# Two transformer blocks, float32, one core: layer 0's scale and shift alone ahead of the context pass, on four 32-column tiles of TensorE; its gate during the context heads

## The reference, cut to what matters

```python
for l in range(DEPTH):                                  # DEPTH = 2
    sh_l, sc_l, g_l = jnp.split(jax.nn.silu(c) @ w_mod[l] + b_mod[l], 3, axis=-1)
    sh_c, sc_c, g_c = jnp.split(jax.nn.silu(c_ctx) @ w_mod[l] + b_mod[l], 3, axis=-1)
    hl = xl * (1.0 + sc_l[:, None, :]) + sh_l[:, None, :]
    hc = xc * (1.0 + sc_c) + sh_c
    parts_c = jnp.split(hc @ w_in[l], SPLIT_POINTS, axis=-1)
    ...                                                 # conv, heads, pooling of ctx and x
    xl_new = _layernorm(DEEPNORM_ALPHA * xl + g_l[:, None, :] * out_l, ln_g[l], ln_b[l])
    xc = _layernorm(DEEPNORM_ALPHA * xc + g_c * out_c, ln_g[l], ln_b[l])
```

## Time and profile before

| what | value |
|---|---|
| time, median of 3 runs | 3728.88 us (3725.71 to 3730.09) |
| span of the profiled execution | 3719.5 us |
| PE busy | 3467.2 us, 93% of the span |
| DVE busy | 2288.1 us, 62% |
| ACT busy | 1303.7 us, 35% |
| DMA moved | 516.21 MB, mean 139 GB/s |

### The profile page before, as it was taken

How to read it: one execution, slowest core, us unless ns; L and a number is a source line. 1 busy time by engine, 2 the same in 40 slices (tenths; PEclk the granted TensorE clock), 3 DMA queues, 4 the chain that set the end, 5 groups by cost and what they waited for, 6 DMA issues and landing times.

```text
span 3719.5 us, 48605 instructions
## 1 busy us (share of the span) xinstructions
PE 3467.2 (93%) x16800; PEld 2732.9 (73%) x16800; DVE 2288.1 (62%) x2909; ACT 1303.7 (35%) x1730; POOL 209.9 (6%) x396
## 2 busy tenths in 40 slices
PE   8699999899999999999799999999997998898996
PEld 2299989678777777878588777767785777687784
DVE  6455565886767764656655566665655888554433
ACT  0145544432334343225522334342326222344323
POOL 1000000000000000110000000000110000000000
PEclk9799999999999999998899999999998999999998
DMA  9844445445223222654554222221652222221231
GB/s 379 267 169 168 166 157 218 143 176 189 105 85 111 99 84 81 234 195 152 187 192 161 105 95 107 104 83 71 217 201 91 80 90 85 80 79 62 103 115 65
DMA packets 95158, 516.21 MB, mean 139 GB/s; under 512 B 11536, under 2 KB 11568, under 8 KB 55760
## 3 DMA queue, kind: packets, MB, share of 16 engines
q1 hardware_dynamic: 51328, 343.95, 25.4%
q0 software_dynamic: 43728, 170.91, 13.3%
HBM read 492.80 MB, written 22.02 MB: 138 GB/s over the span
## 4 chain that ended last, share of the span: by engine, by line
PE 72%; DVE 10%; issue 6%; DVEq 4%; DMA 4%; ACT 3%; ACTq 1%; POOL 0%; SPq 0%; POOLq 0%; PEldq 0%
PE acc L946 20%; PE acc L947 19%; PE acc L948 19%; DVE xy L1739 5%; PE S L1007 3%; PE pv L1041 2%; DVEq L1738 2%; PE S L1136 2%; DVE w_lo L1274 1%; PE misc L1118 1%; PE S L1015 1%; DMA bias_d<-evt 1%; PE S L1009 1%; DMA xy<-in_wm 1%; DVE gates L1321 1%
## 5 line engine op out<-in xcount | busy, mean ns | idle before, releaser
L946 PE MATMUL acc<-h_hi,w_hi 128*128 128x512 f32 (+1 forms) x4736 | 1747.3, 369 | 142.5 <-DVE h_lo L1280 67.6
L947 PE MATMUL acc<-h_lo,w_hi 128*128 128x512 f32 (+1 forms) x4736 | 1713.4, 362 | 0.0
L948 PE MATMUL acc<-h_hi,w_lo 128*128 128x512 f32 (+1 forms) x4736 | 1711.8, 361 | 0.0
L946 PEld LDWEIGHTS acc<-h_hi,w_hi 128*128 128x128 f32 x4736 | 908.5, 192 | 337.4 <-issue 126.2
L948 PEld LDWEIGHTS acc<-h_hi,w_lo 128*128 128x128 f32 x4736 | 909.4, 192 | 135.3
L947 PEld LDWEIGHTS acc<-h_lo,w_hi 128*128 128x128 f32 x4736 | 910.5, 192 | 132.0 <-issue 6.3
L1274 DVE TENSOR_TENSOR w_lo<-raw,w_hi 128x2048 fp32r<-128x2048 f32 x296 | 677.0, 2288 | 270.9 <-ACT w_hi L540 266.0
L540 ACT ACTIVATE w_hi<-raw 128x2048 fp32r<-128x2048 f32 x296 | 564.7, 1908 | 6.9 <-DVEq L1265 6.2
L540 ACT ACTIVATE ev<-acc 128x512 f32<-128x512 f32 (+1 forms) x210 | 110.8, 532 | 1255.9 <-PE acc L948 1222.7
L1321 DVE SCALAR_TENSOR_TENSOR gates<-gates,csil 128x512 f32<-128x512 f32 x568 | 412.2, 750 | 82.8 <-DMA gates<-in_wm 48.1
L1423 DVE TENSOR_REDUCE small<-S 128x2 f32<-128x1536 f32 (+1 forms) x80 | 123.4, 1543 | 309.7 <-PE S L1009 304.4
(11 more groups left out here) (199 smaller groups left out, 2160.2 us busy)
## 6 DMA issues: line engine op xcount, KB each, us to landing
raw<-in_w SPq DMA_DIRECT2D x296, 1024.0 KB, 4.8
gates<-in_wm POOLq DMA_DIRECT2D x216, 512.0 KB, 4.4
xy<-in_wm SPq DMA_DIRECT2D x32, 1024.0 KB, 10.0
x_d<-xy POOLq DMA_DIRECT2D x2, 4096.0 KB, 14.0
vtok<-in_wm POOLq DMA_DIRECT2D x8, 512.0 KB, 7.2
qb<-x_d POOLq DMA_DIRECT2D x16, 256.0 KB, 3.1
kb<-x_d POOLq DMA_DIRECT2D x16, 256.0 KB, 3.8
out_y<-xy POOLq DMA_DIRECT2D x4, 1024.0 KB, 4.1
```

Of the source, the lines that this page charges most:

```text
L946: mm(o, w_hi[:, w], h_hi[:, x], start=n == 0, stop=False)
L947: mm(o, w_hi[:, w], h_lo[:, x], start=False, stop=False)
L948: last = mm(o, w_lo[:, w], h_hi[:, x], start=False, stop=n == len(ks) - 1)
```

## The change

Four things change.

1. **Opening.** The 32 loads of 1 MB now hold scale (16), then shift (16), one block of 128 inputs x 2048 outputs each, from an array of its own, `in_wm0`. For each PE makes four matmuls of 512 columns, one into each quarter of 32 partitions of the same bank (`mod0_step`); the stationary operand is a table `csil0` of 32 columns, of which two hold the vectors and 30 are zero. After 16 steps ACT copies the whole bank out, and four transposes give the columns (`mod0_transposes`). Two weight tiles are loaded ahead of the last eight.
2. **Gate.** Its 16 loads, two per context head, are issued by SP between the loads of weight tiles 0 and 1 of the head, into slots 0 and 1 of `xy`, after a wait that PE has used the slot's last content. PE uses them behind tile 3 of that head; a copy, four transposes and two additions finish it after the last head. PE's loop over the context heads is unrolled. The old path on POOL, DVE and PE is gone.
3. **Bias table.** It is prepared in `kb` and stored from there. POOL issues the store behind the context tokens, as soon as DVE is ready, and DVE waits for it ahead of the context heads; ACT no longer waits.
4. **Rope table.** It is loaded behind the tokens of pass `a`, since its place holds `csil0`.

```diff
+M0_SLOTS = 4
+M0_STEPS = 2 * KT
...
+        csil0 = rope[:, 0:KT * 32]
+        mod0_sums = [S[:, MC * n:MC * (n + 1)] for n in range(2)]
+        mod0_cols = (misc, pv)
+        gate0_row = gates[:, 0:MC]
...
@@ SP
-            def mod0(i):
-                for s in range(4):
-                    sp.wait_ge(m0_used, shown(m0_used, At(s - 3, 4, i)))
-                    sp.dma_start(xy[:, s * D:(s + 1) * D].rearrange("p (t n) -> p t n", t=2),
-                                 A["wm"][bass.ds(i * 8 + 2 * s, 2)].rearrange("t p n -> p t n")).then_inc(m0_landed[s], 16)
-            loop(sp, 0, MOD0_CHUNKS, mod0)
+            for e in range(M0_STEPS):
+                if e == M0_STEPS - 8:
+                    for p in range(2):
+                        load(j_at("cconv", 0, p), w0[p:p + 1])
+                s = e % M0_SLOTS
+                if e >= M0_SLOTS:
+                    sp.wait_ge(m0_used, shown(m0_used, e - M0_SLOTS + 1))
+                sp.dma_start(xy[:, s * D:(s + 1) * D], A["wm0"][e:e + 1]).then_inc(m0_landed[s], 16)
...
+            def chead(i):
+                for p in range(4):
+                    load(j_at("chead", i, p), w0[bass.ds(i * 4 + (16 + p), 1)])
+                    if p == 0:
+                        for s in range(2):
+                            sp.wait_ge(m0_used, shown(m0_used, At(M0_STEPS - 1 + s, 2, i)))
+                            sp.dma_start(xy[:, s * D:(s + 1) * D], A["wm0"][bass.ds(i * 2 + (M0_STEPS + s), 1)])\
+                                .then_inc(m0_landed[s], 16)
+            loop(sp, 0, N_HEADS, chead)
@@ POOL
-                             (evt[0:16, 0:384], A["negmask"])):
+                             (kb[0:16, 0:384], A["negmask"])):
                 pool.dma_start(dst, src).then_inc(consts, 16)
-
-            def gates0(i):
...
-            loop(pool, 0, 4, gates0)
             for dst, src in ((edge[:], A["edge"]),
                              (work[:, 0:KT * CTX].rearrange("p (k t) -> p k t", t=CTX), A["ctxT"])):
                 pool.dma_start(dst, src).then_inc(late_consts, 16)
-            pool.wait_ge(mod_used, shown(mod_used, 4 * MOD_TILES))
-            pool.dma_start(rope, A["rope"]).then_inc(rope_land, 16)
             pool.wait_ge(setup_dve, shown(setup_dve, 3))
             pool.dma_start(bias_d[0:16 * P * 384].rearrange("(h q n) -> h q n", q=P, n=384),
-                           evt[0:16, 0:384].unsqueeze(1).broadcast_to([16, P, 384])).then_inc(bias_st, 16)
+                           kb[0:16, 0:384].unsqueeze(1).broadcast_to([16, P, 384])).then_inc(bias_st, 16)
@@ ACT
-            loop(act, 1, MOD0_CHUNKS // 2, mod0)
+            act.wait_ge(m0_used, shown(m0_used, KT))
+            f(ev[0][:], mod0_sums[0]).then_inc(m0_row, 1)
             hi(At(0))
+            act.wait_ge(m0_used, shown(m0_used, 2 * KT))
+            f(ev[1][:], mod0_sums[1]).then_inc(m0_row, 1)
             act.wait_ge(dve_phase, shown(dve_phase, after("setup")))
             act.wait_ge(late_consts, shown(late_consts, 32))
-            act.wait_ge(bias_st, shown(bias_st, 16))
@@ ACT, after the loop of heads
+                if c == "c":
+                    act.wait_ge(m0_used, shown(m0_used, 3 * KT))
+                    f(gate0_row, mod0_sums[1]).then_inc(m0_row, 1)
@@ PE
+            def mod0_step(e, slot):
+                n, k = e // KT, e % KT
+                landed = e // M0_SLOTS + 1 if n < 2 else M0_STEPS // M0_SLOTS + (e - M0_STEPS) // 2 + 1
+                pe.wait_ge(m0_landed[slot], shown(m0_landed[slot], 16 * landed))
+                to = mod0_sums[min(n, 1)]
+                for q in range(4):
+                    last = mm(to[32 * q:32 * (q + 1), :], csil0[:, 32 * k:32 * (k + 1)],
+                              xy[:, slot * D + MC * q:slot * D + MC * (q + 1)], start=k == 0, stop=k == KT - 1)
+                last.then_inc(m0_used, 1)
...
                             weight_tile(j_at(phase, i, p), a_at(phase, i, p), T, H_AT[c + ".h"])
+                            if c == "c" and p == 3:
+                                for s in range(2):
+                                    mod0_step(M0_STEPS + 2 * i + s, s)
...
+                    mod0_transposes(2, S[:, 3 * MC:4 * MC], gate0_row)
@@ DVE
+                if c == "c":
+                    dve.wait_ge(bias_st, shown(bias_st, 16))
...
-            loop(dve, 1, 4, mod0)
+            mod0_add(0, 1)
+            one_plus((0, 1))
             lo(At(0))
...
+            mod0_add(1, 0)
             phase_done("setup")
```

More of the change, by code:

```diff
@@ L69 @@
     _at += _i * _t
-MOD_OF = {"mod0": ((0, 1), 32), "aconv": ((2, 3), 0), "ahead": ((2, 3), 16), "aout": ((2,), 32),
+MOD_OF = {"aconv": ((2, 3), 0), "ahead": ((2, 3), 16), "aout": ((2,), 32),
           "bconv": ((4,), 0), "bhead": ((4,), 16), "bout": ((4,), 32)}
@@ L190, in build @@
         mraw_landed = [sem(f"mraw_landed{n}") for n in range(2)]
-        gate0_landed = [sem(f"gate0_landed{n}") for n in range(4)]
         mod_used = sem("mod_used", 4)
@@ L363, in stream, with cconv @@
                     loop(sp, 0, n_iter, body)
-            def mod0(i):
-                for s in range(4):
-                    sp.wait_ge(m0_used, shown(m0_used, At(s - 3, 4, i)))
-                    sp.dma_start(xy[:, s * D:(s + 1) * D].rearrange("p (t n) -> p t n", t=2),
-                                 A["wm"][bass.ds(i * 8 + 2 * s, 2)].rearrange("t p n -> p t n")).then_inc(m0_landed[s], 16)
-            loop(sp, 0, MOD0_CHUNKS, mod0)
-            w0, w1, w2 = A["w0"], A["w1"], A["w2"]
-            for c in "ca":
-                for phase, t0 in (("conv", 0), ("head", 16), ("pool", 48), ("out", 56)):
-                    stream(c + phase, w0, t0)
+            w0, w1, w2 = A["w0"], A["w1"], A["w2"]
+            for e in range(M0_STEPS):
[6 more added lines that the diff above has]
+                sp.dma_start(xy[:, s * D:(s + 1) * D], A["wm0"][e:e + 1]).then_inc(m0_landed[s], 16)
+            def cconv(i, first=0):
+                for p in range(first, 4):
+                    load(j_at("cconv", i, p), w0[bass.ds(i * 4 + p, 1)])
+            cconv(0, first=2)
+            loop(sp, 1, N_CONV, cconv)
+            def chead(i):
[7 more added lines that the diff above has]
+            loop(sp, 0, N_HEADS, chead)
+            stream("cpool", w0, 48)
+            stream("cout", w0, 56)
+            for phase, t0 in (("conv", 0), ("head", 16), ("pool", 48), ("out", 56)):
+                stream("a" + phase, w0, t0)
             def kv(i):
@@ L481, in _ @@
                            A["xT"][:, KT // 2:]).then_inc(x_land, 16)
+            pool.dma_start(rope, A["rope"]).then_inc(rope_land, 16)
             residual("c", "cout", A["ctxT"])
@@ L968, in reduce_mod, with mod0_transposes @@
                 last.then_inc(mod_red, 1)
+            def mod0_step(e, slot):
[7 more added lines that the diff above has]
+                last.then_inc(m0_used, 1)
+            def mod0_transposes(n, to, row):
+                pe.wait_ge(m0_row, shown(m0_row, n + 1))
+                for s in range(MOD_COLS):
+                    last = nc.tensor.transpose(to[:, P * s:P * (s + 1)], row[:, P * s:P * (s + 1)], ident[:])
+                last.then_inc(m0_cols, 1)
             def conv(c):
@@ L1066, in heads @@
                 step(1, norm=False, half=1)
-                loop(pe, 1, N_HEADS // 2, two_steps)
+                if c == "c":
+                    for i in range(1, N_HEADS // 2):
+                        two_steps(i)
+                    mod0_transposes(2, S[:, 3 * MC:4 * MC], gate0_row)
+                else:
+                    loop(pe, 1, N_HEADS // 2, two_steps)
                 step(N_HEADS, proj=False)
@@ L1310, in mod_tiles @@
                             dve.drain()
-                        if kk == 0 and phase == "mod0":
-                            dve.wait_ge(gate0_landed[t % 4], shown(gate0_landed[t % 4], At(t // 4, 2, i).times(16) + 16))
-                        elif kk == 0:
-                            landed = (m - 4 * MOD_TILES).half.times(16) + 16
+                        if kk == 0:
+                            landed = m.half.times(16) + 16
                             dve.wait_ge(mraw_landed[m.odd], shown(mraw_landed[m.odd], landed))
@@ L1625, in _, with mod0_add @@
             ts(csil[:], t2[:, 0:48], 0.5, None, ALU.mult)
+            ts(csil0.rearrange("p (k n) -> p n k", n=32)[:, 0:2, :],
+               t2[:, 0:2 * KT].rearrange("p (n k) -> p n k", n=2), 0.5, None, ALU.mult)
             dve.drain()
             dve.sem_inc(setup_dve, 1)
-            def mod0(i):
-                mod_tiles("mod0", i, range(MOD_TILES))
-                mod_columns("mod0", i)
-            mod0(0)
+            def mod0_add(n, what):
+                dve.wait_ge(m0_cols, shown(m0_cols, n + 1))
+                at = mod0_cols[n] if n < 2 else S[:, 3 * MC:4 * MC]
+                for w in range(2):
+                    tt(modc[:, 48 * w + 16 * what:48 * w + 16 * (what + 1)].rearrange("p (q s) -> p q s", q=4),
```

(2 more changed lines are left out.)

79 lines of the change are left out of this document (22 added, 57 removed).

## The result

| kernel | median | runs | ratio to before, 95% interval |
|---|---|---|---|
| before | 3729.49 us | 3725.71 to 3732.84 | |
| changed | 3774.96 us | 3770.09 to 3776.72 | 1.0124 [1.0109, 1.0138] |

The change makes the kernel 45.5 us slower. The forecast was 27 us slower, in a range that holds the result. Its signs were right in both parts (the opening shorter, the heads longer); its size was short by 18.5 us.

A forecast was written before the change was run, and what follows sets the result against it. PE, busy for 93% of the span, was taken to bound the kernel. Opening -50 us and context heads +77 us gave +27 us on a 3719.5 us span, with 9.4 us around it: 3756 us, range 3722 to 3783 us.

The forecast's parts named there:

- The opening: Before the context pass: modulation starts at 123.5 us in place of 173.8 us, 50 us gained (39 to 61).
- The store's cost of 19 us: In the opening: the bias store running beside the loads costs them 19 us, between bounds of 8 and 30 us.
- The four tiles: Modulation matmuls on PE: four 32-column tiles run side by side, 0.9 to 1.1 us a step, 1.9 us per context head.
- The rival of tiles in series: Opening and context heads: the tiles don't run side by side at all; 3790 us, chance 0.07.
- the rival of a partial overlap: Modulation matmuls: a second record holds up the next tile's, 3.9 us per head, 8 us in all; 3764 us, chance 0.10.
- The heads: Context heads: gate loads and their wait delay weight tile 1, 8.6 us per head; with all terms 77 us (60 to 95).
- The clock: Tile 1 after PE's idle gap in seven heads: lower clock costs 1.7 us each (0 to 2.4), 12 us.
- what finishes the gate: After the eighth context head: a copy on ACT, four transposes and two additions that PE and DVE wait for, 1.8 us.
- What lies around the span: Whole kernel: the median, 3728.9 us, lies 9.4 us above the 3719.5 us span, taken as what lies around it.
- The wait is covered: Context heads: weight tile 1 comes early enough despite the queue wait, heads cost only 17 us; 3696 us, chance 0.11.
- The store takes only its bytes: Opening and heads: the store costs loads only its bytes and the clock stays up; -61 + 65, 3733 us, chance 0.13.
- The store excludes the loads: Opening: the bias store holds the loads up, gain only 39 us; 3767 us, chance 0.13.

## Why the prediction was right, and where its size was off

**The opening, right.** Forecast -50 us, measured -51.3. Each step stood: the last load at 119 us (by 118), the start at 123.5 us (122.5). The store's cost of 19 us, taken between the bounds 8 and 30 from the one row that showed a load beside it, was 19.7 us when taken away and 19.9 us from the changed kernel's own rates. The loads had 149 GB/s beside the store where the forecast had 121 GB/s for 30 us. Part of this is luck. The row from 164 to 172 us was taken for what a load gets beside the store, but the same load had got nothing at all from 150.5 to 163.7 us. The earlier trace rows say so: 104 GB/s in all, with a tile load pending. Had the loads of the opening been held up like that one, the cost would have been nearer the upper bound.

**The four tiles, right.** 1.9 us per head forecast; the time between tile 3 and the next tile 0 on PE grew by 2.0 us. The rival of tiles in series (6.9 us) and the rival of a partial overlap (3.9 us) are excluded by the records, and the kernel with one column tile shows what the first would have looked like. The partial rival was built on what the Trainium skill states in "TensorE: Matmul & The Clock Gate", section on packing small matmuls, that matmuls start and end strictly in program order. A matmul here is two records, 0.43 us apart; four matmuls' first records start within 0.02 us of each other, ahead of the first one's second record. Matmul by matmul that is still in order, and the page's remark, there, that tiles start about 4 ns apart is near the 7 ns of this trace. What the trace does not bear out is the rival's reading, that a second record holds up the next tile's matmul. In the kernel with one column tile the order itself does not hold: the second step's first matmul starts at 309.77 us, ahead of the first step's fourth, at 310.62 us.

**The heads, right in mechanism and too small.** The step that was mis-sized is "a load lands after 4.8 us, each further megabyte 2.5 us later", with its tile 1 landing 10.9 us after the end of tile 3. It landed 12.2 to 13.2 us after it. In the head shown, the first gate load took 5.4 us, and the two behind it landed 3.1 and 2.8 us later each. One cause is in the trace: the load of tile 2, issued 0.6 us behind tile 1's, is a fourth megabyte in flight that the term left out. From 296.5 to 307.5 us the engines moved 369 GB/s, 4.06 MB; the three transfers that had landed by then are only 3.15, and 0.7 MB are tile 2's. The wait for data was 8.6 us per head in place of 6.7: 60 us against 47 + 1.3.

**The clock, too small.** "1.7 us for each, between 0 and 2.4: 12 us". It was 17.4 us, 2.5 per head, a little above my upper bound. The term priced only tile 1's own matmuls, and for them it was exact: they lost 1.72 us on average, 12.0 us in seven heads. The lower level begins earlier than the tile: the transposes and the scores ahead of it run under it too, and they are on the path. These 5.4 us the sum put at nothing. With 12 us too little for the data and 5.4 us too little for the clock, 0.5 too little for the gate's matmuls and 1.3 too much for what finishes the gate (0.5 us against 1.8), the terms come within 0.5 us of the heads' 94.3 us against 77.

**The range.** Its ends do not follow from the sum. The largest gain against the smallest loss is 3728.9 - 61 + 60 = 3728 us, not 3722, and the upper loss with a late landing is 3728.9 - 39 + 95 = 3785 us, not 3783. The result lies inside either way.

**What lies around the span, wrong without harm.** I read the 9.4 us between the median and the span as time outside the span. The changed kernel's runs have 1.5 us between time and span in every one (3776.72 and 3775.2 us for the profiled one). The other 8 us were that the profiled execution of the kernel before was a short one: with 1.5 us around its span it took about 3721 us, less than any of the runs beside the change (3725.71 us and more). The forecast is the same either way.

**The rivals.** "The wait is covered" (3696 us) was the right price for the wrong kernel: it is what the change gives with the loads behind tile 3's, 3695 us. "The store takes only its bytes" fell with 19.7 us against 8. "The store excludes the loads" fell for the opening: the loads kept 149 of 423 GB/s beside it. It was the prediction's reading of what the Trainium skill states in "DMA: Bandwidth & Descriptors", section on queues, rings and completion order: that an engine takes turns between queues only after a whole packet. The page gives no figure for what such turns cost. In the opening they cost more than the bytes and less than the whole time; but the rival is what happens, for 10 to 13 us, to a single load that is issued into a running store.

**Still open.** Whether tile 1's load would land earlier with tile 2's held back was not tried. The stretch behind tile 60, 4 to 11 us longer in every other kernel than in the profiled execution before, was not fully told apart from what one execution differs from another. And it is open why a load that meets a running store moves nothing at first.

## What to carry to other kernels

A wait in a DMA queue is paid by the load behind it, not by the one that it is for: put the load that has to wait behind the last one that is urgent, and the same bytes and the same wait cost nothing (80 us here). A stall behind which the granted clock falls costs more than its length; count what runs at the lower clock ahead of the next tile as well as the tile. And a slow store is best cut into pieces that each fit into the slack of one load: whole, it cost 19.7 us beside a full queue and 8 us beside a half-empty one, in eight pieces 0.3 us.

## What the runs showed of the hardware

- Four matmuls of 512 columns (float32, two records each) in four 32-column tiles take 1.94 us at the lower clock (the row at 117.99 us); two such steps take 1.92 us at the full one (the row at 294.91 us). In one tile the records follow each other by 0.43 us.
- A matmul for another column tile can start ahead of older ones that still wait for their own tile: in the one-tile kernel 16 records of two steps take 5.4 us instead of 6.9.
- A store whose source lies in 16 partitions, read 128 times over, moves 104 GB/s alone while the DMA engines read as full. It leaves loads that are under way 35% of their rate (149 of 423 GB/s). A load issued while it runs alone moved nothing for 10.5 us (the store held back) and for 13.2 us (the kernel before). A share of 1.01 says that the engines are taken, not what they move.
- Matmuls without purpose in a gap of 8 us kept the granted clock at 1.00 there and behind it, and made the kernel 16 us faster.
